# A three-product matmul of split weights: column units that stream high and low activations together, a reordered conformer norm and narrower pooling products

## What is computed

```python
def squared_relu_mlp(xn, w1, w2):
    h = jax.nn.relu(xn @ w1)
    return (h * h) @ w2

# conformer: a, gate = split(xn @ pw1_w + pw1_b); h = a * sigmoid(gate)
h = lax.conv_general_dilated(h, dw_w, padding=[(30, 0)], feature_group_count=1024) + dw_b
h = silu(layer_norm(h, ln_w, ln_b)) @ pw2_w + pw2_b

# hybrid layer
y_a = short_conv_mixer(b_a, c_a, x_a, conv_w, w_a_out)      # (b * conv3(c * x)) @ w_a_out
y_p = multiscale_pool_mixer(u_p, w_pool, pool_scale)        # windows 2, 4, 8, 16 over tokens
y_t = windowed_gqa(q, k, v, rel_bias, sink) @ w_attn_out
merged = sigmoid(ga) * y_a + sigmoid(gp) * y_p + sigmoid(gt) * y_t
x = x + merged @ w_o
gate, up = split(rms_norm(x, g_ffn) @ w_gu)
return x + (silu(gate) * up) @ w_down
```

## Time and profile before

| | us |
|---|---|
| median of 3 runs | 2462.28 (2461.33 to 2462.77) |
| profiled execution | 2464.05 |
| its span | 2461.8 |
| VectorE busy | 1480.9 |
| ScalarE busy | 1115.7 |

### The profile page before, as it was taken

The page is one execution under the profiler, slowest core; times in us unless marked ns, Lnnn a source line. Parts: engine busy times, 40 slices in busy tenths (PEclk is TensorE's granted clock), DMA queues, the critical chain, the costliest instruction groups (busy, mean ns, idle before and its releaser), DMA issues.

```text
span 2461.8 us, 35215 instructions
## 1 busy us (share of the span) xinstructions
PE 2380.7 (97%) x14772; PEld 2112.3 (86%) x14772; DVE 1480.9 (60%) x1443; ACT 1115.7 (45%) x1107; POOL 135.7 (6%) x182
## 2 busy tenths in 40 slices
PE   7999999979999899999999999999999999999998
PEld 6787998958988689877879978899899898998997
DVE  6666546966456654576564556755654567466454
ACT  5444444235436543454453445533444455334343
POOL 0000090500000000000000000000000000000000
PEclk9999999989999999999999999999999999999999
DMA  6443654214453255434545444435444454443543
GB/s 261 180 188 142 230 218 171 103 69 177 171 204 137 103 201 205 172 155 165 194 182 205 171 160 180 161 130 214 167 172 187 171 197 167 155 192 147 201 169 121
DMA packets 68369, 424.17 MB, mean 172 GB/s; under 512 B 10832, under 2 KB 11120, under 8 KB 22432
## 3 DMA queue, kind: packets, MB, share of 16 engines
q1 hardware_dynamic: 58752, 399.83, 42.0%
q0 software_dynamic: 9504, 22.71, 2.9%
HBM read 421.40 MB, written 5.28 MB: 173 GB/s over the span
## 4 chain that ended last, share of the span: by engine, by line
PE 90%; DVE 6%; ACT 3%; issue 1%; DMA 0%; POOL 0%; DVEq 0%; ACTq 0%
PE pair L695 19%; PE pair L697 18%; PE pair L696 18%; PE acc L695 10%; PE acc L696 9%; PE acc L697 9%; DVE work L1940 2%; DVE w_lo L1652 1%; PE pair L738 1%; PE acc L1067 1%; PE acc L1094 1%; PE acc L1083 1%; PE pair L1131 1%; ACT act_hi L1240 1%; PE pair L864 1%
## 5 line engine op out<-in xcount | busy, mean ns | idle before, releaser
L1652 DVE TENSOR_TENSOR w_lo<-raw,w_hi 128x2048 fp32r<-128x2048 f32 (+1 forms) x404 | 860.8, 2161 | 226.2 <-ACT w_hi L1185 225.2
L1185 ACT ACTIVATE w_hi<-raw 128x2048 fp32r<-128x2048 f32 (+1 forms) x404 | 713.1, 1804 | 156.3 <-PE acc L697 126.0
L695 PE MATMUL pair<-act_hi,w_hi 128*128 128x256 f32 x2496 | 709.9, 284 | 2.5 <-DVE w_lo L1652 2.5
L697 PE MATMUL pair<-act_hi,w_lo 128*128 128x256 f32 x2496 | 706.3, 283 | 0.0
L696 PE MATMUL pair<-act_lo,w_hi 128*128 128x256 f32 x2496 | 706.2, 283 | 0.0
L695 PEld LDWEIGHTS pair<-act_hi,w_hi 128*128 128x128 f32 x2496 | 478.7, 192 | 10.6 <-issue 8.5
L696 PEld LDWEIGHTS pair<-act_lo,w_hi 128*128 128x128 f32 x2496 | 478.8, 192 | 2.1
L697 PEld LDWEIGHTS pair<-act_hi,w_lo 128*128 128x128 f32 x2496 | 478.7, 192 | 0.0
L695 PE MATMUL acc<-w_hi,hid_hi 128*128 128x512 f32 x848 | 335.4, 396 | 6.2 <-DVE hid_lo L1705 6.2
L696 PE MATMUL acc<-w_lo,hid_hi 128*128 128x512 f32 x848 | 331.3, 391 | 0.0
L697 PE MATMUL acc<-w_hi,hid_lo 128*128 128x512 f32 x848 | 330.6, 390 | 0.0
(11 more groups left out here) (225 smaller groups left out, 2436.8 us busy)
## 6 DMA issues: line engine op xcount, KB each, us to landing
raw<-weights SPq DMA_DIRECT2D x356, 1024.0 KB, 6.6
raw<-weights SPq DMA_DIRECT2D x48, 512.0 KB, 6.3
work<-bias_scratch POOLq DMA_DIRECT2D x32, 192.0 KB, 2.8
bias_scratch<-bias_rows POOLq DMA_DIRECT2D x4, 1024.0 KB, 22.6
work<-ret_gn_w POOLq DMA_DIRECT2D x8, 256.0 KB, 5.2
work<-ret_gn_b POOLq DMA_DIRECT2D x8, 256.0 KB, 5.9
work<-table_pool POOLq DMA_DIRECT2D x2, 1024.0 KB, 7.4
work<-table_decay POOLq DMA_DIRECT2D x2, 768.0 KB, 6.7
```

The costliest lines, as they stand in the source:

```text
L695: mm(o, a_hi, b_hi, start=start, stop=False)
L697: return mm(o, a_lo, b_hi, start=False, stop=stop)
L1185: run(w_hi[slot][:, part], raw[slot][:, part], ACT.Copy).then_inc(hi_done, 1)
L1652: tt(w_lo[slot][:, part], raw[slot][:, part], w_hi[slot][:, part].bitcast(F32), ALU.subtract).then_inc(lo_done, 1)
```

## The change

`act` and `hid` become single tensors that hold the high and the low part side by side. A new column unit streams both parts in one matmul of 512 columns with the high weights, and the high part in one of 256 with the low weights. Each piece has its own pair; the low half of a pair is copied to SBUF by ScalarE (`low_half`) and added by VectorE (`join`). It is used by A1 and later units of both feed-forwards and by 12 units of each hybrid layer: the second q unit, attention output (2), pooling gate (2), fourth c, x (1), b (2), ga (2), w_a_out (2).

```diff
+            def unit_both(both=act, quarter=None):
+                for piece in range(2):
+                    o = open_pair()
+                    h, l = open_piece(piece, 2 * P)
+                    for n in range(2):
+                        if (piece, n) == (0, 1) and quarter is not None:
+                            quarter()
+                        b, cs = 512 * n, slice(n * P, (n + 1) * P)
+                        for k in range(KT):
+                            mm(tiles(o[:, b:b + 512]), h[:, k, cs], both[:, :, k, :], start=k == 0, stop=False)
+                            last = mm(o[:, b:b + SEQ], l[:, k, cs], both[:, 0, k, :], start=False, stop=k == KT - 1)
+                    close(last)
...
-                    unit_f(middle=turn_first if first else None)
+                    unit_both(quarter=turn_first if first else None)
...
+            def low_half(dst):
+                o, _, _ = use()
+                run(tiles(dst), o[:].rearrange("p (n h t) -> p n h t", n=2, h=2)[:, :, 1, :],
+                    ACT.Copy).then_inc(gate_ready, 1)
...
+            def join(dst, low):
+                o, done, _ = use()
+                await_gate()
+                return tt(tiles(dst), o[:].rearrange("p (n h t) -> p n h t", n=2, h=2)[:, :, 0, :], tiles(low),
+                          ALU.add).then_inc(done, 1)
```

In the first feed-forward VectorE now does Relu and square in one operation per piece behind the sum. In the second, Silu works on the joined gate and the product on the joined up part. The weights of the next unit are split between the pieces. In the hybrid layers, at b and likewise at w_a_out, on ScalarE and VectorE:

```diff
                 for i in range(2):
-                    next_unit()
-                    use()
-                    await_drained(S.p - 1)
-                    round_chunk(hid_hi[:, four(i), :])
+                    low_unit(gate[:, i, :])
+                    if i == 1:
+                        await_value()
+                        round_chunk(hid_hi[:, four(0), :])
+                ahead(S.u + 1)
+                await_value()
+                round_chunk(hid_hi[:, four(1), :])
...
                 for i in range(2):
-                    next_unit()
-                    o, done, slot = use()
-                    tt(tiles(val[:, S.c % 2, :]), tiles(o[:]), H_CV[:, four(i), :], ALU.mult).then_inc(done, 1)
+                    join_unit(gate[:, i, :], product)
+                    if i == 1:
+                        ahead(S.u + 1)
                     rest_hid(4 * i)
```

The pooling products stream only tokens that a group's window can reach, and the conformer's norm is computed with a shift (minus the mean of tiles 0 and 1, `C_NEG`), so that the sums of values and squares grow as tiles come:

```diff
-                        for s in range(2):
-                            last = mm(o[:, (k % 4) * SEQ:(k % 4 + 1) * SEQ], H_UP[:, s, k * P:(k + 1) * P],
-                                      H_POOL[:, k // 2, s, :], start=s == 0, stop=s == 1)
+                        for s, t0, t1, start, stop in ((0, 0, P - reach, True, True), (1, P - reach, SEQ, True, False),
+                                                       (0, P - reach, P + reach, False, True)):
+                            last = mm(o[:, b + t0:b + t1], H_UP[:, s, k * P:(k + 1) * P],
+                                      H_POOL[:, k // 2, s, t0:t1], start=start, stop=stop)
...
+                order = (5, 0, 1, 2, 3, 4, 7, 6)
                 for k in order:
+                    if k in (5, 0, 7):
+                        pe.wait_ge(squared, S.due("squared"))
+                    if k == 6:
+                        pe.wait_ge(conv_ready, 5)
                     last = mm(o[:, 0:SEQ], C_MEAN, C_Y[:, k, :], start=k == order[0], stop=k == order[-1])
+                    last = mm(o[:, 512:512 + SEQ], C_MEAN, C_SQ[:, k, :], start=k == order[0], stop=k == order[-1])
...
+                tt(C_Y[:, 0:5, :], C_Y[:, 0:5, :], C_NEG.unsqueeze(1).broadcast_to([P, 5, SEQ]), ALU.add).then_inc(centred, 1)
                 convolve_one(6)
...
+                stt(C_M, o[:, 512:512 + SEQ], EPS, C_DSQ, ALU.add, ALU.subtract).then_inc(done, 1)
```

More of the change, by code:

```diff
@@ L899, in conformer @@
                 unit_f()
+                pe.wait_ge(conv_ready, 2)
+                o = open_pair()
+                shift_use = S.p - 1
+                for k in range(2):
+                    last = mm(o[:, 0:SEQ], C_MEAN, C_Y[:, k, :], start=k == 0, stop=k == 1)
+                last.then_inc(pair_full, 1)
                 convolve(1)
@@ L1543, in head_chunk, with low_unit, sigmoid @@
                     round_chunk(hid_hi[:, four(i), :])
[L1545 to L1547 removed]
+                def low_unit(dst):
+                    due = S.split == S.u + 1
+                    for piece in range(2):
+                        if due:
+                            split_piece(S.u + 1, piece)
+                        piece_done(piece)
+                        low_half(dst[:, 512 * piece:512 * (piece + 1)])
+                    S.split += 1 if due else 0
+                    S.u += 1
+                def sigmoid(dst):
+                    for piece in range(2):
+                        await_value()
+                    run(dst, dst, ACT.Sigmoid).then_inc(opened, 1)
+                o, done, slot = result(True)
+                run(H_Q[:, four(0), :], tiles(o[:]), ACT.Copy).then_inc(done, 1)
+                low_unit(H_Q[:, four(1), :].rearrange("p k t -> p (k t)"))
                 next_unit()
@@ new lines, in mlp1, with mlp2, first_a, make @@
+                mlp_walk(dve, S, FFN1_CHUNKS, {"u": 4, "split": 4, "p": 4, "c": 2, "v": 2, "g": 4}, first_a, make, last_b)
+            def mlp2():
+                release()
+                def first_a():
+                    o, done, slot = result(True)
+                    await_gate()
+                    tt(val[:, S.c % 2, 0:512], o[:, 512:1024], gate[:, slot, 0:512], ALU.mult).then_inc(done, 1)
+                    rest_hid(4 * (S.c % 2), 2)
+                def make(first):
+                    at = S.c % 2
+                    if not first:
@@ new lines, in value_done, with scaled_pool @@
+                def value_done(part):
+                    S.v += 1
+                    nc.vector.memset(small[:, 123:124], 0.0).then_inc(value_ready, 1)
+                def scaled_pool(i, dst):
+                    o, done, slot = use()
+                    for n in range(4):
+                        cs = slice(SEQ * n, SEQ * (n + 1))
+                        last = stt(dst[:, cs], o[:, cs], colv(f"pool_scale{layer}", 4 * i + n), H_SIGP[:, i, cs],
+                                   ALU.mult, ALU.mult)
+                    last.then_inc(done, 1)
```

375 lines of the change are left out of this document (224 added, 151 removed).

## The result

| | before | changed |
|---|---|---|
| median of 16 runs | 2462.36 | 2467.05 |
| span of the profiled execution | 2461.8 | 2465.3 |
| TensorE busy | 2380.7 | 2369.1 |
| VectorE busy | 1480.9 | 1590.6 |

The account below looks back on a forecast made before the run. TensorE, busy 97% of 2461.8 us, was taken as the bound; -28.8 - 4.4 - 7.6 + 31.0 = -9.8 from 2464.05 gave 2454.25, and 1.77 less for the median 2452.5 us; 8-in-10 range 2437 to 2468.

Parts of the forecast that it names:

- Column units: 72 merged units: three matmuls per k become two, 0.0125 us less per step, 28.8 us off, bounds 0 to 31.
- The sign that it gave: From the first column unit on: above 0.354 us per k step, 15 us of gain lost, the kernel is slower.
- Low halves and sums in the loops: ScalarE copies (0.60 us) and VectorE sums (0.69) per half unit hide; second feed-forward's slack of 0.55 stays.
- Rival (d): Loops' slack used up by two more waits per unit: 10 to 14 us cost, about 2465 us; chance 0.11.
- The two places in each hybrid layer: Depthwise gate and output product: late rounding of chunk 0 makes TensorE rest 6.06 and 5.45 us.
- Rival (a): Hybrid-layer rests do not come because VectorE or ScalarE gets by otherwise: 2421.5 us; chance 0.08.
- Clock behind a rest: Lower clock after each long TensorE rest in the hybrid layers costs 2.0 us, bounds 0 and 3.4.
- Pooling: Hybrid layers' pooling products, 24 narrower for 16 full: gain 2.2 us per layer (1.3 to 3.1), 4.4 in both.
- Conformer: Reordered norm behind tile 6's convolution lets TensorE start row units 7.6 us earlier, bounds 4 to 10.
- Rival (e): Conformer gains nothing, as sums delay tile 6 or the tail ends elsewhere: 2460.1 us; chance 0.10.

Follow-up runs that it names:

- grouped order: Changed kernel with the 16 matmuls of 512 columns of a piece first, then its 16 of 256: 2454.4 us (one run).
- single-stretch operand: Changed kernel with each 512-column product of a column unit streaming 512 neighbouring columns in place of high and low of one k: 2468.59 us (one run).
- the experiment: Changed kernel with the conformer's convolution tail and norm as before: 2474.91 us, 1.0050 of before.
- In fours: Changed kernel with four matmuls of 512 columns, then four of 256, and so on: 2463.7 us (one run).

## Why the prediction was wrong, step by step

**Column units: this is the step that failed.** It put "Per k three matmuls (0.3597 us) become one of 512 and one of 256 columns (0.2273 + 0.1199 = 0.3472)". Both durations were right, each for a run of its own width. Alternating, the pair took 0.353 us in most units, and 0.347 in some. The gain was 17.2 us in place of 28.8. The grouped order gave the forecast's unit (11.10 us for 11.11), and the single-stretch operand gave nothing, so the size was lost where the two widths alternate at the slow pace, and not to the operand. Why they have a slow pace is open. The result lies inside the stated bounds (0 to 31; with its 0.2267 the upper one is 30), but the step took nearly the top end as "nearest in form", while no row of before showed two widths in turn. The sign that it gave, 0.354 us per k, was also set too far out: by its own sum of -9.8 the gain is gone at 0.3515 (9.8 us over 2304 steps), and 0.353 was measured.

**Low halves and sums in the loops.** Right: the turns of the second feed-forward show no wait of TensorE, even with units of 11.10 us. Rival (d) had the right time, 2465, by a cause that did not come about.

**The two places in each hybrid layer.** Right in place, cause and size: 5.69 us for 6.06, 5.19 for 5.45, released by the sum and by the low weights as forecast. One move on ScalarE took away all four rests and 31.2 us, 28.6 of them at these places. Rival (a) is out.

**Clock behind a rest.** 1.6 and 1.5 us for the 2.0 taken from the earlier trace rows. At the ga unit part of the time at the lower level (from 1675.0) fell into the rest itself, where it costs nothing.

**Pooling.** 2.8 us for 4.4. A layer took 5.34 us. The upper bound had been 5.4, with the narrow matmuls at 0.26 us each; the value taken was the middle of the bounds, and the dear end was right.

**Conformer.** 8.4 us in the trace and 7.9 in the experiment (7.0 at the conformer itself) for 7.6. Rival (e) is out. The tail behind tile 6 was 10.1 us for 10.6.

**Untouched stretches.** 3.8 us that no term had. Part of it is chance: the 16 runs of the changed kernel differ by 2.5 us among themselves.

With the merge at its forecast size the sum would have been about 2455. The sign hung on a difference of terms of 41 off and 31 on, so an error of 12 in the largest was enough, and the chance of 0.68 for faster was too high for that.

## What to carry to other kernels

Where two engines work through hand-written queues, look for every instruction that the other engine waits for and that stands behind work on data not yet made: here one rounding behind one more unit's low halves, at two places in each of two layers, cost some 29 us, and moving it turned the change from 0.2% slower into 1.1% faster. A cost per instruction read from runs of equal width holds for runs of equal width; where a change brings two widths in turn, bound it apart, and keep the same widths together if accumulation allows any order. And when gain and loss are of one size, the forecast is their difference, and its range must carry the error of the larger.

## What the runs showed of the hardware

- fp32r matmuls with a weight load each: 0.1199 us at 256 columns and 0.2273 at 512 in runs of one width. In turn the pair took 0.353 or 0.347 us, at a granted clock of 1.00 in both. In fours a step took 0.350, in sixteens 0.347. Row units of 512 columns take 10.94 us behind a slow unit and 10.91 behind a fast or a grouped one.
- Once a pace is there it mostly lasts until other work comes, over up to seven column units in a row. In every trace looked at here it was the fast one behind the pooling products and the transposes of the first units, and in the feed-forwards of the changed kernel the slow one behind each row unit; behind a rest of 1.24 or 5.69 us it was either. Why is open: the weight loads in the records keep step with the matmuls in both cases, and no run here separates how the engine fetches from how it loads.
- A matmul operand of two stretches of 256 columns costs no more than one of 512 neighbours (11.29 us a unit both ways).
- Plain f32 products with 2176 of 4096 columns in half as many instructions again took 5.34 of 6.72 us, not the 3.57 of their columns' share: narrow ones cost more than their columns.
- The rests were worse than their length: 10.9 us of waits in a layer cost 3.1 us of clock on the spot.
